# A triangular inverse of five levels run in one piece on the matrix engine of a recurrent mixer kernel

## What is computed

```
def step(state, inp):
    r_t, w_t, k_t, v_t, a_t, b_t = inp
    sa = jnp.einsum('bhij,bhj->bhi', state, a_t)
    state = (state * w_t[:, :, None, :]
             + sa[..., :, None] * b_t[..., None, :]
             + v_t[..., :, None] * k_t[..., None, :])
    y = jnp.einsum('bhij,bhj->bhi', state, r_t)
    return state, y
```

```
y = ((y - mean) * lax.rsqrt(var + GN_EPS)).reshape(b, s, RWKV_WIDTH)
y = y * lnx_w + lnx_b
...
h = h + gate[:, None, :] * y
return rms_norm(h, final_gain)
```

## Time and profile before

| | us |
|---|---|
| median of 3 runs | 2938.42 (2935.45 to 2938.51) |
| profiled execution, its own time | 2935.95 |
| its span in the trace | 2934.2 |
| mean granted clock of TensorE | 0.989 |

### The profile page before, as it was taken

The page is one execution under the profiler, slowest core; times in us unless marked ns, Lnnn a source line. Parts: engine busy times, 40 slices in busy tenths (PEclk is TensorE's granted clock), DMA queues, the critical chain, the costliest instruction groups (busy, mean ns, idle before and its releaser), DMA issues.

```text
span 2934.2 us, 75567 instructions
## 1 busy us (share of the span) xinstructions
PE 2816.7 (96%) x31013; PEld 2339.9 (80%) x31013; DVE 1559.7 (53%) x3137; ACT 1087.6 (37%) x2515; POOL 477.3 (16%) x627
## 2 busy tenths in 40 slices
PE   5999999999889999999999999999999999999996
PEld 5777778777578888888888888888888888888884
DVE  2411211111256666666666666666666666666665
ACT  2232332332034433433444433333443333334442
POOL 3201011011012112111111112111111112111120
PEclk9999999999899999999999999999999999999998
DMA  8623313322100000000000000000100000000100
GB/s 337 237 71 100 114 64 107 104 75 93 58 16 23 30 23 23 23 23 23 30 30 23 30 23 23 23 23 23 38 23 30 23 23 23 23 23 25 36 17 23
DMA packets 67732, 153.09 MB, mean 52 GB/s; under 512 B 4026, under 2 KB 37391, under 8 KB 65423
## 3 DMA queue, kind: packets, MB, share of 16 engines
q1 hardware_dynamic: 63134, 130.08, 12.6%
q0 software_dynamic: 1680, 11.01, 0.9%
q10 hardware_dynamic: 2656, 7.87, 0.7%
HBM read 98.61 MB, written 50.33 MB: 51 GB/s over the span
## 4 chain that ended last, share of the span: by engine, by line
PE 52%; DVE 11%; ACT 6%; issue 5%; DVEq 0%; DMA 0%; ACTq 0%
PE bank L894 25%; PE bank L943 12%; PE bank L930 8%; PE bank L1062 2%; DVE SV L1421 2%; ACT sig L1133 1%; ACT sig L1132 1%; DVE LA L1446 1%; DVE mix L1337 1%; PE bank L904 1%; DVE t L1366 1%; ACT UV L1223 1%; DVE LA L1442 1%; DVE kk L1373 1%; DVE t L1374 1%
## 5 line engine op out<-in xcount | busy, mean ns | idle before, releaser
L894 PE MATMUL bank<-xT,w 128*128 128x128 f32 x8704 | 1106.9, 281 | 7.4 <-DMA xT<-xt_dram 7.4
L894 PEld LDWEIGHTS bank<-xT,w 128*128 128x128 f32 x8704 | 1012.3, 192 | 43.4 <-issue 8.4
L1165 ACT ACTIVATE XX<-bank 128x256 f32<-128x256 f32 x320 | 122.9, 384 | 909.0 <-PE bank L943 896.6
L339 PE MATMUL bank<-xT,w 128*128 128x256 f32 x2048 | 451.9, 382 | 4.9 <-ACT xT L447 4.9
L339 PEld LDWEIGHTS bank<-xT,w 128*128 128x128 f32 x2048 | 392.3, 192 | 65.7 <-issue 10.5
L1431 DVE TENSOR_TENSOR XV<-bank,level_mask 128x256 f32<-128x256 f32 x320 | 132.9, 423 | 327.5 <-PE bank L943 318.3
L930 PE MATMUL bank<-wo,Y 128*128 128x512 f32 x512 | 232.0, 596 | 4.6 <-DVE Y L1391 4.6
L365 PE MATMUL bank<-wo,yc 128*128 128x512 f32 x512 | 227.2, 598 | 0.9 <-DVE yc L663 0.9
L943 PEld LDWEIGHTS bank<-XX,AI 64*64 64x64 f32 x5120 | 163.5, 136 | 63.8 <-issue 52.4
L943 PE MATMUL bank<-XX,AI 64*64 64x64 f32 x5120 | 185.5, 222 | 5.1 <-DVE XX L1464 5.1
L365 PEld LDWEIGHTS bank<-wo,yc 128*128 128x128 f32 x512 | 97.0, 192 | 111.9 <-issue 109.6
(11 more groups left out here) (178 smaller groups left out, 3603.1 us busy)
## 6 DMA issues: line engine op xcount, KB each, us to landing
x_in<-in_x SPq DMA_DIRECT2D x16, 1024.0 KB, 7.2
xr<-in_x SPq DMA_DIRECT2D x32, 512.0 KB, 4.3
xt_dram<-xT SPq DMA_DIRECT2D x32, 512.0 KB, 8.4
h_dram<-xr SPq DMA_DIRECT2D x32, 512.0 KB, 2.6
xT<-xt_dram SPq DMA_DIRECT2D x32, 512.0 KB, 3.3
gate_row<-h_dram SPq DMA_DIRECT2D x32, 512.0 KB, 3.3
out<-gate_row SPq DMA_DIRECT2D x32, 512.0 KB, 2.6
w<-in_w_in POOLq DMA_DIRECT2D x8, 1088.0 KB, 11.1
```

What stands on the lines that cost most here:

```text
L339: last = nc.tensor.matmul(bank[t // 2][:, (t % 2) * T1:(t % 2 + 1) * T1], w1[:, k, t * P:(t + 1) * P], xT[:, k, :], start=(k == 0), stop=( ...
L894: last = nc.tensor.matmul(bank[b][:, q * P:(q + 1) * P], w2[:, k, (t0 + q) * P:(t0 + q + 1) * P], xT[par][:, k, :], start=(k == 0), stop=( ...
L1165: s(nc.scalar.activation(XX[j][:, k].rearrange(flat), bank[2 + j][:, 256 * k:256 * (k + 1)], ACT.Copy), xx_ready, hold=False)
```

## The change

All five levels run behind one another with no projection slots and no output projection between them. Each half of a level is cut into four pieces, one for each chunk j and pair of pairs a (8 records each), and each piece has a bank of its own (2, 3 for chunk 0; 5, 6 for chunk 1), its first product in columns 0 to 127 and its second in 128 to 255. ScalarE's copies and VectorE's masks go by pieces of 128x128 too (20 instead of 10 of each in a block), the transposes stay whole. What stood between the levels goes elsewhere: four slots more ahead of them (`fill(10)`), eight behind, two between `from_state(0)` and `solve(0)`, one more before `solve(1)`; both halves of the output projection and `low_rank` directly behind the levels. On VectorE shift 0, group scale, tanh and group gate stand ahead of level 0; shift 2 and `key` move ahead of `take_r(0)`, `new_key` ahead of `take_r(1)`. On ScalarE the exponentials and sigmoids of the low-rank part and `take_group(2)` stand ahead of `take_u(0)`. GpSimd's copies wait for the end of the last level instead of for the group gate.

The diff, cut to its core (the counts of `lx_ps`, `xx_ps`, `xv_ready` and `xx_ready` double with the pieces):

```diff
+PIECES = [(j, a) for j in range(NC) for a in range(2)]
+def level_bank(j, a):
+    return bank[(2, 5)[j] + a]
+def piece(i, j, a):
+    return (i * NC + j) * 2 + a + 1
 GROUPS = [(12, 1, 0), (0, 4, 1), (4, 4, 0), (8, 4, 1), (13, 4, 0)]
...
             last.then_inc(out_ps.sem, 1)
-        def inverses(fill, other):
-            def heads(o, lhsT, rhs):
-                for p in range(NP):
+        def inverses():
+            def heads(o, lhsT, rhs, a):
+                for p in (2 * a, 2 * a + 1):
                     for e in range(2):
                         h = half(e)
-                        last = nc.tensor.matmul(o[h, p * HD:(p + 1) * HD], lhsT[h, p], rhs(h, p), start=True, stop=True)
+                        c = (p - 2 * a) * HD
+                        last = nc.tensor.matmul(o[h, c:c + HD], lhsT(h, p), rhs(h, p), start=True, stop=True)
                 return last
-            s.wait(v_ready, 1)
             for i in range(LV):
-                for j in range(NC):
+                for j, a in PIECES:
                     if i:
-                        s.wait(xx_ready, NC * (i - 1) + j + 1)
+                        s.wait(xx_ready, piece(i - 1, j, a))
                     else:
...
                     let_through(pe, pe_gate)
-                    heads(bank[5 + j][:, 0:256], AI[j], lambda h, p: XX[j][h, 0, p]).then_inc(lx_ps.sem, 1)
-                fill(2)
-                for j in range(NC):
-                    s.wait(xv_ready, NC * i + j + 1)
+                    heads(level_bank(j, a)[:, 0:128], lambda h, p: AI[j][h, p], lambda h, p: XX[j][h, 0, p], a)\
+                        .then_inc(lx_ps.sem, 1)
+                for j, a in PIECES:
+                    s.wait(xv_ready, piece(i, j, a))
                     if i:
...
                     let_through(pe, pe_gate)
+                    o = level_bank(j, a)[:, 128:256]
                     if i < LV - 1:
-                        heads(bank[2 + j][:, 0:256], XX[j][:, 1], lambda h, p: XV[j][h, p]).then_inc(xx_ps.sem, 1)
+                        last = heads(o, lambda h, p: XX[j][h, 1, p], lambda h, p: XV[j][h, p], a)
                     else:
-                        heads(bank[2 + j][:, 256:512], XV[j], lambda h, p: XX[j][h, 1, p]).then_inc(xx_ps.sem, 1)
-                fill()
-                if i in (2, 3):
-                    other(i - 2)
+                        last = heads(o, lambda h, p: XV[j][h, p], lambda h, p: XX[j][h, 1, p], a)
+                    last.then_inc(xx_ps.sem, 1)
         def from_state(j):
...
         def solve(j):
-            s.wait(xx_ready, NC * (LV - 1) + j + 1)
+            s.wait(xx_ready, piece(LV - 1, j, 1))
             s.wait(r_ready, j + 1)
...
                             last.then_inc(gram_ps.sem, 1)
-            fill(6)
+            fill(10)
+            s.wait(v_ready, 1)
             s.wait(bt_ready, 2)
-            inverses(fill, (lambda h: None) if first else out_half)
+            inverses()
+            if not first:
+                out_half(0)
+                out_half(1)
+            if ahead:
+                s.wait(xx_ready, piece(LV - 1, 0, 1))
+                low_rank()
+            fill(8)
+            s.wait(xx_ready, piece(LV - 1, 1, 1))
             from_state(0)
-            if ahead:
-                s.wait(xx_ready, NC * LV)
-                low_rank()
+            fill(2)
             solve(0)
...
             from_state(1)
-            fill(1)
+            fill(2)
             solve(1)
...
         def take_inverse(i):
-            for j in range(NC):
-                s.wait(xx_ps, NC * i + j + 1)
-                k = i // (LV - 1)
-                s(nc.scalar.activation(XX[j][:, k].rearrange(flat), bank[2 + j][:, 256 * k:256 * (k + 1)], ACT.Copy),
+            k = i // (LV - 1)
+            for j, a in PIECES:
+                s.wait(xx_ps, piece(i, j, a))
+                s(nc.scalar.activation(XX[j][:, k, 2 * a:2 * a + 2].rearrange(flat), level_bank(j, a)[:, 128:256], ACT.Copy),
                   xx_ready, hold=False)
...
                 take_group(n + 1, 0)
-            take_inverse(0)
-            if ahead:
                 exp_tanh()
-            take_inverse(1)
+            for i in range(LV):
+                take_inverse(i)
             if not first:
...
             s(nc.scalar.activation(rgate[:, :, :], rg[:, :, :], ACT.Exp, scale=-1.0), erg_ready)
-            take_inverse(2)
             if ahead:
                 take_group(n + 1, 1)
-            take_inverse(3)
             s.wait(gclamp_ready, 1)
...
             s(nc.scalar.activation(rgate[:, :, :], rgate[:, :, :], ACT.Exp, scale=-1.0), gsig_ready)
-            take_inverse(4)
             if not first:
...
             if ahead:
+                exp_low_rank(0)
+                exp_low_rank(1)
+                sigmoid(0)
+                sigmoid(1)
                 take_group(n + 1, 2)
-            if ahead:
-                exp_low_rank(0)
             take_u(0)
-            if ahead:
-                exp_low_rank(1)
             s.wait(y_ps, 1)
...
             if ahead:
-                sigmoid(0)
                 key_scale()
-                sigmoid(1)
             take_u(1)
...
             s(copy(prev[:, :, 0:1], prev[:, :, T2:T2 + 1], ones[:, 0:MIX].unsqueeze(2)), carry_ready)
-            if not first:
-                pv.block(n - 1)
-                pv.wait(y2_ready, 1)
+            s.wait(xx_ready, piece(LV - 1, 1, 1))
             for j in range(NC):
...
         def level(i):
-            if i:
-                for j in range(NC):
-                    s.wait(xx_ready, NC * (i - 1) + j + 1)
+            for j in range(NC):
+                if i:
+                    s.wait(xx_ready, piece(i - 1, j, 1))
                     s(nc.vector.transpose(XX[j][:, 1].rearrange(flat), XX[j][:, 0].rearrange(flat)), xt_ready, hold=False)
-            for j in range(NC):
-                s.wait(lx_ps, NC * i + j + 1)
-                s(nc.vector.tensor_tensor(XV[j][:, :, :], per_head(bank[5 + j][:, 0:256]),
-                                          level_mask[i][:, :].unsqueeze(1).broadcast_to([P, NP, HD]), ALU.mult), xv_ready, hold=False)
+                for a in range(2):
+                    s.wait(lx_ps, piece(i, j, a))
+                    s(nc.vector.tensor_tensor(XV[j][:, 2 * a:2 * a + 2, :], per_head(level_bank(j, a)[:, 0:128]),
+                                              level_mask[i][:, :].unsqueeze(1).broadcast_to([P, 2, HD]), ALU.mult), xv_ready, hold=False)
         def run(n, first, ahead, par):
...
                 s(nc.vector.transpose(XX[j][:, 0].rearrange(flat), XX[j][:, 1].rearrange(flat)), x1_ready, hold=False)
-            if not first:
-                group_scale(1 - par)
-            level(0)
-            if not first:
-                group_gate()
             if ahead:
                 shift(n + 1, 0)
-            level(1)
+            if not first:
+                group_scale(1 - par)
             if ahead:
                 tanh()
-            level(2)
+            if not first:
+                group_gate()
+            for i in range(LV):
+                level(i)
             s.wait(erg_ready, 1)
             s(nc.vector.tensor_scalar(rgate[:, :, :], rgate[:, :, :], LN_MAX, None, ALU.min), gclamp_ready)
-            level(3)
             if not first:
...
                 shift(n + 1, 1)
-            level(4)
             if not first:
...
             s(nc.vector.tensor_tensor(rgate[:, :, :], rgate[:, :, :], rg[:, :, :], ALU.mult), rgate_ready)
-            take_r(0)
             if not first:
...
             if ahead:
+                clamp(0)
+                clamp(1)
                 shift(n + 1, 2)
                 key()
-                clamp(0)
+            take_r(0)
+            if ahead:
+                decay_sum()
             new_state(0)
             if ahead:
-                clamp(1)
+                new_key()
             take_r(1)
-            if ahead:
-                decay_sum()
-                new_key()
             new_state(1)
...
```

16 lines of the change are left out of this document (8 added, 8 removed).

## The result

The changed kernel takes 3013.97 us (median; 3008.88 to 3015.16) against 2937.28 (2935.45 to 2938.51): a ratio of **1.0266**, 95% interval 1.0254 to 1.0278. It is slower by 77 us where I had forecast 12 us less, and 3014 lies outside the range of 2903 to 2960. The profiled execution took 3015.13, with a span of 3013.1 against 2934.2: 78.9 more.

What follows compares the result with a forecast made beforehand. The prediction took TensorE's program order as the bound. Its terms, -3.05 + 2.6 + 1.1 - 1.2 = -0.55 us a block, gave -17 over 31 blocks, with +3 in the last -14: 2925 us, range 2903 to 2960.

Steps and rivals of the forecast that it cites:

- Part 1: TensorE's changes between 64x64 and 128x128 matmuls: nine pairs at 0.38 us go, about one returns, -3.05 us a block.
- Part 2: Levels without projection cover: 2.18 us a level, run ending at 11.6 against 9.02 of issue, +2.6 us a block.
- Rival (a): VectorE's masks slower than taken: a level 2.39 us instead of 2.18, with tanh no faster about 2974 us; 13%.
- Rival (b): TensorE's clock falls to 0.50 after idling in level 0 or ahead of solve(0): 2952 to near 2980 us; 13%.
- (c): Wait at the bonus product stays, VectorE being late another way: +1.2 us a block, 2962 us; 7%.
- (d): Each added semaphore increment takes 0.028 us of TensorE: 0.56 us a block, gain gone, 2938 to 2942 us; 7%.
- (e): More gain: VectorE not late at level 0, or shift 2 in time for solve(0): 2891 to 2903 us; 8%.
- Part 3: New TensorE wait at solve(0) for shift 2, key and take_r(0) on VectorE: +1.1 us a block (0.6 to 1.6).
- Part 4: Wait at bonus product L918 goes, as GpSimd's BK ends before new_state(1)'s second half: -1.2 us a block (0 to -1.3).
- The last block: No slots for cover; final norm and square come between output projection and take_r(0): some +3 us once, an estimate.

Runs made afterwards that it cites:

- e3: Kernel before with only the order of VectorE and ScalarE behind take_r(0) changed, new_key staying behind take_r(1): 2894.23 us, ratio 0.9870.
- e11: e6 with two slots each behind levels 1 and 3, four fewer behind the run, decay_sum behind new_state(0), new_key behind take_r(1): 2945.35 us, ratio 1.0048.
- e7: Changed kernel with 12 projection slots ahead of the levels instead of 10 and 6 behind them instead of 8: 3012.84 us, ratio 1.0279.
- e5: Kernel before with only the four pieces, their banks, 20 more increments a block and smaller operations, slots in the old place: 2937.24 us, ratio 1.0016.
- e6: Changed kernel with take_r(0) ahead of shift 2 and the key step on VectorE: 2966.14 us, ratio 1.0117.
- e1: Changed kernel with 64 more semaphore increments in TensorE's program, once, ahead of the loop over blocks: 3018.28 us, ratio 1.0288.
- e2: Changed kernel with 128 more semaphore increments in TensorE's program, once, ahead of the loop over blocks: 3041.01 us, ratio 1.0366.
- e10: Kernel before with 64 more semaphore increments in TensorE's program, once, ahead of the loop over blocks: 2939.08 us, ratio 1.0020.

## Why the prediction was wrong, point by point

- **What bounds it**: right. TensorE's program order is what counts; e3 took 1.20 us out of a block and got 37 of 38 us back.
- **Part 1, changes of shape**: the price is about right. In e11 2.13 us pass from the last matmul of level 1 or 3 to the first of the next; its 16 projection matmuls at 0.111 and one step of 0.028 are 1.80, which leaves 0.33 for a pair, against my 0.38. With that and 0.89 for each of its four slots, e11's run is 12.4 net, and an undisturbed run of the changed kernel takes 12.3 to 12.5.
- **Part 2, the step that failed.** Without a stop the run takes 12.3, not 11.6: level 0 has 3.0 to 3.2 instead of 2.87, a level 2.25 instead of 2.18, and 0.1 to 0.2 are small gaps. That alone would have cost 0.7 x 31 = 22 us, and the forecast would have been 2947, inside the range. The rest has no term in my sum: 0.8 us a block of stops inside the run, and 0.6 between the run and the output projection (16.2 us of L939 in the waits, over some 26 blocks). In e11, where the stops are gone, that stretch is 12.08 with four slots fewer, and 15.64 with them added, as forecast. The budget of the 28 steady blocks closes: my sum, -15; the run mis-sized, +20; stops, +39; three falls of the clock (below), some +6; together 50, measured 49.3. I had taken 0.028 us a matmul from runs of 32 and multiplied it by 320, as if a rate read in 1 us held for 9; the instruction queue stood in the page with 244 packets of 16 KB, and I had not asked what they meant for a stretch of 706 records. Two or three boundaries fall into each run.
- **Rival (a)** pointed the right way at a third of its size: the level came out 0.07 longer, not 0.21, though a mask of 128 columns takes 0.278 us and I had taken 0.30. Which link is longer can be read from the 80 undisturbed levels of the steady blocks: the third mask starts 1.27 us into the level (my sum had 1.29), the third piece of TensorE's second half 0.49 behind it, and the next level 0.49 after that, together 0.98 where I had 0.885. TensorE goes on at the third mask and then has two pieces to issue, not at the fourth with one. In block 0, where there is less beside it, the middle link is 0.40 and the level 2.17; what makes the difference, no run shows. My rate for a mask also had a slip: 0.681 at 512 columns and 0.424 at 256 are 0.996 columns a ns, not 0.96, which changes 0.133 to 0.128 and nothing else. **Rival (b)** came true in a small way: the granted clock fell to 0.50 in three steady blocks for about 3.4 us each. The windows around one of them (us, busy times, PEclk the third number from the end):

```profile
1326.00:1328.00 2.00, 0.56 (x6) 0.30 (x2) 0.61 (x1) 1.89 (x7) 1.24 (x2) 0.95 0.00 0
1328.00:1331.00 3.00, 3.00 (x5) 1.08 (x4) 0.00 (x0) 1.36 (x3) 2.61 (x5) 0.50 0.02 5
```

  0.56 us of work in the 2 us ahead of it: that is the stop in front of the output projection. These blocks took about 2 us more each, 6 in all. In this kernel (b)'s place was right only in that an idle TensorE came first; the idleness was not one of those I had listed. In e7, with the wait of `solve(0)` at 1.7 to 1.9, the clock did fall behind one of the two that (b) names. **(c)** did not happen; **(d)** fell with e5; **(e)** did not happen.
- **Part 3**: right. 1.1 forecast; 1.03 us idle in each block, and e6 removed 1.10 between `from_state(0)` and `solve(0)`:

```profile
1819.08 0.69 DVE L1357 TENSOR_TENSOR kk<-mix,vec 128x512 f32<-128x512 f32 x1
1819.81 0.42 DVE L1419 COPY R<-bank 128x256 f32<-128x256 f32 x1
...
1820.33 0.68 PE L1000 MATMUL bank<-R,XX 64*64 64x64 f32 x16 [1.03 <-issue]
```

- **Part 4**: right. -1.19 us a block; SV's second half 0.87, behind GpSimd's BK and not beside it.

```profile
1832.26 2.63 POOL L1292 TENSOR_TENSOR BK<-k,egi 64x512 f32<-64x512 f32 x2 [8.87 <-ACT egi L1157]
...
1835.24 0.87 DVE L1428 TENSOR_TENSOR SV<-stmp,dend 64x256 f32<-64x256 f32 x2
```

- **The last block**: +15.7 instead of +3. `solve(0)` waits 3.93 there for the final norm in front of `take_r(0)`, 3.3 more than before (0.64): this is the +3. Most of the rest is two stops in the levels, 5.7 together, and the matmuls behind them at half clock (1.92 us for 32 instead of 1.15):

```profile
2946.29 0.53 PE L953 MATMUL bank<-XX,AI 64*64 64x64 f32 x12
2950.07 1.34 PE L953 MATMUL bank<-XX,AI 64*64 64x64 f32 x20 [3.26 <-issue]
2951.20 1.92 PE L953 MATMUL bank<-XV,XX 64*64 64x64 f32 x32
...
2958.84 1.36 PE L953 MATMUL bank<-XX,AI 64*64 64x64 f32 x28 [2.40 <-issue]
...
2973.98 1.12 PE L1000 MATMUL bank<-R,XX 64*64 64x64 f32 x16 [3.93 <-issue]
```

  Blocks 1 and 30 have stops as well, of 3.1 and 2.5 us and of 2.7 (+7.8 and +5.8).
- **The range** was too narrow above: its ends were made of the operations that I had listed. The chance of 0.27 for slower was given to rivals that end at 2980; the largest term, 1.4 us a block, belonged to a resource that none of them named.

**What stays open.** That the stops belong to places 256 instructions apart, and follow a packet of queue 8, is shown (e1, e2, e7, with e10 as control). That the transfer causes the stop is inferred from the order in time, from all 36 ending 2.3 to 2.9 us behind a packet, and from the boundaries with an early packet passing without one; the transfer can't be removed. Why a packet begins early at one boundary and late at the next, and why the stops in blocks 1, 30 and 31 are up to 3.3 us long (the packet of the longest starts 0.6 us into the stop, 2.66 us ahead of its end), no run shows. In its profiled execution e11 is 7 us faster than before in the 28 steady blocks and 16 slower in the rest of the execution, 12 of them in the last block, where nothing covers the run; I tried nothing against that.

## What to carry to other kernels

Look at what is queued on TensorE, not only at what it waits for: a page's instruction queue tells how many instructions it has to be fed, and a stretch of small matmuls that runs for many hundred instructions without a large one between them can be too dense for that supply; projection between the levels was cover for the supply as well as for VectorE. When a rate is read from a group of 32 instructions, it holds for 32; ask what else happens in a stretch ten times as long. And test each part of a large change alone: one part here was worth 38 us by itself (e3), another cost 44 (e6), and neither can be seen in the sum.
